# Splitting 544 token columns as 294 and 250, with one 500-column matmul per weight tile

## The chip, the cores and the metric

The kernel runs on one core of one Trainium2 chip. The metric is the device time of one execution in microseconds (us), median over runs. The engines are TensorE (PE for its matmuls, PEld for its weight loads), VectorE (DVE), ScalarE (ACT), GpSimd (POOL) and SyncE (SP), which issues the DMAs.

## The reference

One decoder layer is computed for 512 prompt tokens and 32 sampled tokens (8 sequences of 4), 544 columns in all. What matters here is that almost all of the work is products of the activations with large float32 weights, to float32 accuracy:

```
proj = rmsnorm(x) @ w_in                    # 2048 -> 4096: pooling inputs, q, k, v
pooled = pool_mix(u, ...)                   # windows 2/4/8/16, then @ w_pool
attn = moba(q, k, v, cache_k, cache_v)      # block-sparse attention, paged cache
x = x + rmsnorm(concat(pooled, attn) @ w_out)          # 2048 -> 2048
gt, up = h @ w_gate, h @ w_up               # h = rmsnorm(x), 2048 -> 5632 each
f = gelu(causal_conv3(gt)) * up
y = x + rmsnorm(f @ w_down)                 # 5632 -> 2048
```

## The kernel before, in words

Activations lie transposed: features on the 128 partitions, the 544 tokens along the free dimension. `act_hi[:, kt]` and `act_lo[:, kt]` hold, for each of 16 slabs of 128 features, the fp32r rounding of the activation and the fp32r rest. `f_hi` and `f_lo` do the same for four slabs of the FFN's inner activation.

Weights come in 724 *units* of 256 KB: two slabs (i = 0, 1) of 128 input features by 256 output features. SP loads a unit into a ring of four slots (`w_raw`). ACT rounds it to fp32r (`split_hi`, L255, into `w_hi`), and DVE subtracts to get the rest (`split_lo`, L261, into `w_lo`). Both run three units ahead of PE (`LEAD = 3`).

A *weight tile* is 128 by 128: a unit has four (i = 0, 1 and output halves mt = 0, 1). For each tile PE forms hi*hi + hi*lo + lo*hi. Each of the three products takes two matmuls of 272 token columns, one into each of two PSUM banks, so six matmuls a tile, each with its own weight load. `group` (L682) does this for the projections before the FFN, with all of mt = 0 before mt = 1 inside a unit. `ff_unit` (L705) does it for the FFN and for the first pair of groups, with i outermost.

A *group* is eight units, which finish 256 output features (mt = 0 and 1) in PSUM. Groups use the banks `ps_acc`, or for `odd = 1` the banks `ps_a` and `ps_b`. When a tile of a group is complete (`acc_done` for mt = 0, `unit_used` for mt = 1), DVE *evicts* it from PSUM to SBUF, mostly multiplied by `rstd`, and increments `acc_free`. PE waits on `acc_free` before the first matmul that overwrites these banks: the previous group's eviction (`prev=1`) where successive groups share `ps_acc`, the one before that (`prev=2`) where they alternate.

The stages in order:

- Input projection, 16 groups. The first two are interleaved (`pair_groups`). Groups 4 to 11 carry the score products with the cached keys between their units (L747), groups 12 to 15 the products with the cached values (L859). Between them stands the prompt attention.
- Four small pooling products, then the output projection: eight groups, evicted by `mix_tiles` (L1223). All but the first use `ps_acc` one after the other.
- The FFN: 11 chunks. A chunk has four gate/up groups (mt = 0 is the gate, mt = 1 the up projection), whose evictions are `gate_tail` (L1278 to L1301), and then 16 units of the down projection in four steps `down(d)`, whose results are added into `acc` (L1335, L1337). The chain of `gate_tail` goes from DVE to ACT and back three times (L599, L602, L606) and ends with `f_lo` (L1301), for which the down projection waits (`f_split`). Only then does DVE go on to the `split_lo` of the next group's fourth unit.
- Root mean square, residual, store.

The order on each engine is the program's order. The mean square of a normalisation (`sum_squares`, L716) is put into columns 272 to 407 of the `ps_acc` banks, beside group results that take columns 0 to 271.

## Time and profile before

| | |
|---|---|
| median of 3 runs | 2845.67 us (2845.61 to 2847.35) |
| span of the profiled execution, first to last instruction | 2843.8 us |
| left of the median around the span | 1.9 us |
| PE busy | 2740.9 us (96%), 19408 matmuls |
| DVE busy | 1172.0 us (41%) |
| ACT busy | 710.6 us (25%) |
| DMA | 122 GB/s over the span |

The profiled execution's own time is not given apart from its span; the runs shown are other executions, and their median is 1.9 us above the span. Busy shares of PE count overlapping matmuls once, and the end of a matmul is modelled, so the pace of matmuls is read from their starts.

### The profile page before, as it was taken

Reading aid. Unit: us, or ns where it says so; the run is one execution under the profiler, and the core shown is the slowest. Engines: PE = TensorE matmul, PEld = TensorE weight load, DVE = VectorE, ACT = ScalarE, POOL = GpSimd, SP = SyncE. Lnnn points to the kernel's source line nnn. Section 1 sums busy time; section 2 is a strip of 40 time slices with the busy share of each in tenths; the row PEclk is TensorE's granted clock in tenths of the full one; section 3 lists DMA queues with packets and bytes.
Section 4 is the critical chain, followed back from the end, with each engine's and each line's share of the span. In section 5 each row is a group of like instructions: output and inputs, shape, how many; then the busy total and the mean of one; then the engine's idle time right before and its main releaser. Section 6 shows DMA issues by size and latency. Waiting matters only on the chain.

```text
span 2843.8 us, 51136 instructions
## 1 busy us (share of the span) xinstructions
PE 2740.9 (96%) x19408; PEld 2416.9 (85%) x19408; DVE 1172.0 (41%) x1852; ACT 710.6 (25%) x1226; POOL 120.9 (4%) x265
## 2 busy tenths in 40 slices
PE   8999999979999999789999999999999999999994
PEld 8876767654444699789999999999999999999994
DVE  7433222340111433584343434444444343434357
ACT  5211111250111222342222222222222222222231
POOL 3000000000000000130000000000000000000002
PEclk9999999999999999899999999999999999999997
DMA  4455556407777442222222222222322223232321
GB/s 162 138 200 211 207 197 219 152 8 234 242 239 245 147 156 88 59 71 89 86 89 87 86 89 86 87 89 78 96 81 92 85 89 88 87 86 89 87 91 74
DMA packets 146616, 347.23 MB, mean 122 GB/s; under 512 B 16608, under 2 KB 16608, under 8 KB 146048
## 3 DMA queue, kind: packets, MB, share of 16 engines
q1 hardware_dynamic: 144480, 338.35, 37.2%
q0 software_dynamic: 2080, 8.14, 0.8%
q8 instruction: 35, 0.57, 0.1%
q14 instruction: 21, 0.17, 0.0%
HBM read 334.32 MB, written 12.10 MB: 122 GB/s over the span
## 4 chain that ended last, share of the span: by engine, by line
PE 93%; DVE 4%; DVEq 1%; ACT 1%; issue 0%; DMA 0%; POOL 0%; SPq 0%; ACTq 0%; POOLq 0%
PE ps_acc L705 28%; PE ps_acc L682 18%; PE ps_a L705 14%; PE ps_b L705 14%; PE ps_a L747 8%; PE ps_a L859 4%; PE ps_b L859 4%; PE ps_a L682 1%; PE ps_b L682 1%; PE ps_acc L801 1%; DVE act_lo L957 1%; DVE region L1362 0%; DVE w_lo L261 0%; DVE region L1247 0%; DVE region L1366 0%
## 5 line engine op out<-in xcount | busy, mean ns | idle before, releaser
L261 DVE TENSOR_TENSOR w_lo<-w_raw,w_hi 128x512 fp32r<-128x512 f32 x724 | 502.1, 705 | 1217.2 <-ACT w_hi L255 1214.2
L255 ACT ACTIVATE w_hi<-w_raw 128x512 fp32r<-128x512 f32 x724 | 445.5, 628 | 1397.7 <-PE ps_acc L682 475.9
L705 PE MATMUL ps_acc<-act_hi,w_hi 128*128 128x272 f32 x1472 | 308.4, 291 | 33.8 <-DVE act_lo L957 18.9
L705 PE MATMUL ps_acc<-act_lo,w_hi 128*128 128x272 f32 x1472 | 306.9, 290 | 0.0
L705 PE MATMUL ps_acc<-act_hi,w_lo 128*128 128x272 f32 x1472 | 304.8, 288 | 0.0
L682 PE MATMUL ps_acc<-act_hi,w_hi 128*128 128x272 f32 x1280 | 273.6, 295 | 2.0 <-DVE scratch L968 1.1
L682 PE MATMUL ps_acc<-act_hi,w_lo 128*128 128x272 f32 x1280 | 264.6, 288 | 0.0
L682 PE MATMUL ps_acc<-act_lo,w_hi 128*128 128x272 f32 x1280 | 263.9, 288 | 0.0
L705 PEld LDWEIGHTS ps_acc<-act_hi,w_hi 128*128 128x128 f32 x1472 | 232.5, 190 | 36.5 <-issue 22.1
L682 PEld LDWEIGHTS ps_acc<-act_hi,w_hi 128*128 128x128 f32 x1280 | 199.8, 188 | 49.7 <-issue 48.3
L747 PE MATMUL ps_a<-region,q_blk 128*32 128x256 f32 x1024 | 233.2, 382 | 2.3 <-ACT q_blk L423 2.3
L705 PEld LDWEIGHTS ps_acc<-act_hi,w_lo 128*128 128x128 f32 x1472 | 233.4, 190 | 0.0
L705 PEld LDWEIGHTS ps_acc<-act_lo,w_hi 128*128 128x128 f32 x1472 | 233.2, 190 | 0.0
L682 PEld LDWEIGHTS ps_acc<-act_lo,w_hi 128*128 128x128 f32 x1280 | 201.1, 189 | 0.0
L747 PEld LDWEIGHTS ps_a<-region,q_blk 128*32 128x32 f32 x1024 | 108.5, 110 | 108.2 <-ACT q_blk L423 2.5
L682 PEld LDWEIGHTS ps_acc<-act_hi,w_lo 128*128 128x128 f32 x1280 | 199.8, 189 | 0.0
L705 PE MATMUL ps_a<-act_hi,w_hi 128*128 128x272 f32 x736 | 153.4, 290 | 0.0
L705 PE MATMUL ps_b<-act_lo,w_hi 128*128 128x272 f32 x736 | 152.7, 288 | 0.0
L705 PE MATMUL ps_a<-act_lo,w_hi 128*128 128x272 f32 x736 | 152.3, 288 | 0.0
L705 PE MATMUL ps_b<-act_hi,w_lo 128*128 128x272 f32 x736 | 152.0, 288 | 0.0
L705 PE MATMUL ps_b<-act_hi,w_hi 128*128 128x272 f32 x736 | 151.7, 288 | 0.0
L705 PE MATMUL ps_a<-act_hi,w_lo 128*128 128x272 f32 x736 | 151.3, 286 | 0.0
(210 smaller groups left out, 3981.1 us busy)
## 6 DMA issues: line engine op xcount, KB each, us to landing
w_raw<-units SPq DMA_DIRECT2D x724, 256.0 KB, 2.6
region<-kcache SPq DMA_DIRECT2D x128, 512.0 KB, 4.2
region<-vcache SPq DMA_DIRECT2D x128, 512.0 KB, 4.5
region<-xT SPq DMA_DIRECT2D x8, 544.0 KB, 6.7
region<-xT SPq DMA_DIRECT2D x4, 1088.0 KB, 8.4
yT<-region SPq DMA_DIRECT2D x8, 544.0 KB, 2.7
ext_out<-region POOLq DMA_DIRECT2D x8, 339.5 KB, 4.5
kT_out<-scratch POOLq DMA_DIRECT2D x8, 272.0 KB, 5.8
```

What stands on the lines that cost most here:

```text
L255: act.activation(w_hi[:, s], w_raw[:, s], ACT.Copy).then_inc(hi_ready, 1)
L261: dve.tensor_tensor(w_lo[:, s], w_raw[:, s], w_hi[:, s].bitcast(F32), ALU.subtract).then_inc(lo_ready, 1)
L682: mm = pe.matmul(banks(mt, odd)[:, n, 0:HN], w[:, s, i, cols], half(a[:, kt], n), start=kt == 0 and w is w_hi and a is hi, stop=kt == 2 * ...
L705: mm = pe.matmul(banks(mt, odd)[:, n, 0:HN], w[:, s, i, cols], half(a[:, kt], n), start=kt == 0 and w is w_hi and a is hi, stop=kt == 2 * ...
L747: mm = pe.matmul(ps_a[0:HC, quad % 2, s * P:(s + 2) * P], q_blk[:, h * HC:(h + 1) * HC], pages[:, s:s + 2, h * P:(h + 1) * P], start=h == ...
L801: mm = pe.matmul(ps[:, 0, h % 2, kj * P:SEQ], v_tok[:, h, kj], probT[:, kj, kj * P:SEQ], start=kj == 0, stop=kj == 3)
L859: mm = pe.matmul(o[0:HC, n, :], p_seq[:, s % 2, c:c + HC], pages[:, slot, n * 512:(n + 1) * 512], start=pg == 0, stop=pg == PAGES - 1)
L957: dve.scalar_tensor_tensor(act_lo[:, kt], src[:, kt], g[:, kt:kt + 1], act_hi[:, kt].bitcast(F32), ALU.mult, ALU.subtract).then_inc(act_re ...
```

## The change

The columns are split as HA = 294 and HB = 250. `act_hi` and `act_lo` become the two halves of one tensor `act[:, kt, 0 or 1, :]`, so that columns 294 to 543 of the high and of the low part can be streamed by one matmul with 2 x 250 columns against `w_hi`. Its 500 results go side by side into the second bank. The first bank takes the 294 other columns in three matmuls as before. A fifth matmul adds `w_lo` times the high part of the 250 columns into the first 250 of the 500 sums. The second 250 (`b_rest`) are added when the tile is evicted. The interleaved first pairs of groups (32 units, where `sum_squares` needs its columns) and the four pooling products keep the six matmuls (`even=True`). That leaves 688 units with five.

```diff
+HA, HB = 294, 250
-        act_hi = sb("act_hi", [P, KT, NT], F32R)
-        act_lo = sb("act_lo", [P, KT, NT], F32R)
+        act = sb("act", [P, KT, 2, NT], F32R)
+        act_hi, act_lo = act[:, :, 0], act[:, :, 1]
+        rests = scratch[:, 3, 0:2 * HB].rearrange("p (m n) -> p m n", m=2)
+        def sums(mt, odd=0):
+            b = banks(mt, odd)
+            return b[:, 0, 0:HA], b[:, 1, 0:HB], b[:, 1, HB:2 * HB]
+        def products(pe, mt, odd, s, i, a, kt, first, last, even):
+            cols = slice(mt * P, (mt + 1) * P)
+            hi, lo = w_hi[:, s, i, cols], w_lo[:, s, i, cols]
...
+            bank_a, bank_b = banks(mt, odd)[:, 0, 0:HA], banks(mt, odd)[:, 1]
+            pe.matmul(bank_b[:, 0:2 * HB].rearrange("p (x n) -> p x n", x=2), hi, a[:, kt, :, HA:NT],
+                      start=first, stop=False)
+            pe.matmul(bank_a, hi, a[:, kt, 0, 0:HA], start=first, stop=False)
+            pe.matmul(bank_a, hi, a[:, kt, 1, 0:HA], start=False, stop=False)
+            pe.matmul(bank_a, lo, a[:, kt, 0, 0:HA], start=False, stop=last)
+            return pe.matmul(bank_b[:, 0:HB], lo, a[:, kt, 0, HA:NT], start=False, stop=last)
-                            for w, a in ((w_hi, hi), (w_hi, lo), (w_lo, hi)):
-                                for n in range(2):
-                                    mm = pe.matmul(banks(mt, odd)[:, n, 0:HN], w[:, s, i, cols], half(a[:, kt], n),
-                                                   start=kt == 0 and w is w_hi and a is hi,
-                                                   stop=kt == 2 * nu - 1 and w is w_lo)
+                            mm = products(pe, mt, odd, s, i, a, kt, kt == 0, kt == 2 * nu - 1, even)
+            def times_rstd(out, mt, odd=0):
+                (a, b, b_rest), rest = sums(mt, odd), rests[:, mt]
+                dve.tensor_tensor(rest, b_rest, rstd[:, HA:NT], ALU.mult)
+                dve.tensor_tensor(out[:, HA:NT], b, rstd[:, HA:NT], ALU.mult)
+                dve.tensor_tensor(out[:, 0:HA], a, rstd[:, 0:HA], ALU.mult).then_inc(acc_free, 1)
+                dve.drain()
+                dve.tensor_tensor(out[:, HA:NT], out[:, HA:NT], rest, ALU.add)
+            def times_rstd_spread(prompt, sample, mt, odd=0):
+                (a, b, b_rest), rest = sums(mt, odd), rests[:, mt]
+                dve.tensor_tensor(rest, b_rest, rstd[:, HA:NT], ALU.mult)
+                dve.tensor_tensor(prompt[:, HA:SEQ], b[:, 0:SEQ - HA], rstd[:, HA:SEQ], ALU.mult)
+                dve.tensor_tensor(sample, b[:, SEQ - HA:HB].rearrange("p (b l) -> p b l", b=DB), samples(rstd), ALU.mult)
+                dve.tensor_tensor(prompt[:, 0:HA], a, rstd[:, 0:HA], ALU.mult).then_inc(acc_free, 1)
+                dve.drain()
+                dve.tensor_tensor(prompt[:, HA:SEQ], prompt[:, HA:SEQ], rest[:, 0:SEQ - HA], ALU.add)
+                dve.tensor_tensor(sample, sample, rest[:, SEQ - HA:HB].rearrange("p (b l) -> p b l", b=DB), ALU.add)
...
-                    dve.tensor_copy(two(tile_of(acc, 2 * g + mt)), bank(mt, odd)).then_inc(acc_free, 1)
+                    t, (a, b, b_rest) = tile_of(acc, 2 * g + mt), sums(mt, odd)
+                    dve.tensor_copy(t[:, HA:NT], b)
+                    dve.tensor_copy(t[:, 0:HA], a)
+                    dve.drain()
+                    dve.tensor_tensor(t[:, HA:NT], t[:, HA:NT], b_rest, ALU.add).then_inc(acc_free, 1)
...
-                                    o = dve.tensor_tensor(two(t), two(t), bank(mt, i), ALU.add)
-                                o.then_inc(acc_free, 1)
+                                    dve.tensor_tensor(t[:, HA:NT], t[:, HA:NT], b, ALU.add)
+                                    dve.tensor_tensor(t[:, 0:HA], t[:, 0:HA], a, ALU.add)
+                                dve.drain()
+                                dve.tensor_tensor(t[:, HA:NT], t[:, HA:NT], b_rest, ALU.add).then_inc(acc_free, 1)
```

On PE, two weight tiles of the down projection (mt = 0 in `ps_a`, mt = 1 in `ps_b`; `f_hi`, `f_lo` and after the change `f_act` are the FFN's inner activation) stood like this before:

```order
L705 MATMUL ps_a<-f_hi,w_hi 128x272 x2
L705 MATMUL ps_a<-f_lo,w_hi 128x272 x2
L705 MATMUL ps_a<-f_hi,w_lo 128x272 x2
L705 MATMUL ps_b<-f_hi,w_hi 128x272 x2
L705 MATMUL ps_b<-f_lo,w_hi 128x272 x2
L705 MATMUL ps_b<-f_hi,w_lo 128x272 x2
```

and the same two tiles after it:

```order
L298 MATMUL ps_a<-f_act,w_hi 128x500
L300 MATMUL ps_a<-f_act,w_hi 128x294
L301 MATMUL ps_a<-f_act,w_hi 128x294
L302 MATMUL ps_a<-f_act,w_lo 128x294
L303 MATMUL ps_a<-f_act,w_lo 128x250
L298 MATMUL ps_b<-f_act,w_hi 128x500
L300 MATMUL ps_b<-f_act,w_hi 128x294
L301 MATMUL ps_b<-f_act,w_hi 128x294
L302 MATMUL ps_b<-f_act,w_lo 128x294
L303 MATMUL ps_b<-f_act,w_lo 128x250
```

Six matmuls of 272 columns became five with 500, 294, 294, 294 and 250: 1632 columns both times.

On DVE, the tail of a gate/up group (`scratch` holds the conv input, the conv result and the FFN buffer) stood like this before:

```order
L1278 TENSOR_TENSOR scratch<-ps_acc,rstd 128x272
L1279 TENSOR_TENSOR scratch<-ps_acc,rstd 128x240
L1280 TENSOR_TENSOR scratch<-ps_acc,rstd 128x8x4
L1286 TENSOR_TENSOR scratch<-ps_acc,rstd 128x544
L1289 SCALAR_TENSOR_TENSOR scratch<-scratch,region 128x560
```

and after the change:

```order
L998 TENSOR_TENSOR scratch<-ps_acc,rstd 128x250
L999 TENSOR_TENSOR scratch<-ps_acc,rstd 128x218
L1000 TENSOR_TENSOR scratch<-ps_acc,rstd 128x8x4
L1001 TENSOR_TENSOR scratch<-ps_acc,rstd 128x294
L1003 TENSOR_TENSOR scratch<-scratch 128x218
L1004 TENSOR_TENSOR scratch<-scratch 128x8x4
L989 TENSOR_TENSOR scratch<-ps_acc,rstd 128x250
L990 TENSOR_TENSOR scratch<-ps_acc,rstd 128x250
L991 TENSOR_TENSOR scratch<-ps_acc,rstd 128x294
L993 TENSOR_TENSOR scratch<-scratch 128x250
L1332 ISA
L1332 SCALAR_TENSOR_TENSOR scratch<-scratch,region 128x560
```

Four instructions ahead of the first step of the convolution became ten, with a drain inside each of the two parts.

## Rows read from the trace of the kernel before

**Rows 1.** Windows: busy us (count) of PE, PEld, DVE, ACT, POOL; granted clock; DMA.

```profile
122.00:445.00 323.00, 323.00 (x1930) 228.03 (x1928) 94.96 (x148) 52.48 (x94) 6.62 (x12) 1.00 0.59 205
640.00:1000.00 360.00, 359.54 (x1538) 186.26 (x1537) 76.19 (x119) 47.94 (x76) 4.31 (x8) 0.99 0.67 220
1000.00:1180.00 180.00, 176.06 (x1404) 175.64 (x1402) 63.81 (x92) 48.03 (x76) 0.00 (x0) 1.00 0.36 111
1312.00:2800.00 1488.00, 1488.00 (x11871) 1488.00 (x11870) 647.59 (x1044) 394.55 (x628) 24.93 (x159) 1.00 0.29 87
```

**Rows 2.** Chain that ended last: start us, length us, engine, tile, line, count.

```profile
1006.49 168.38 PE ps_acc L682 x1344
...
1645.08 24.12 PE ps_acc L705 x192
```

**Rows 3.** Window in the slow-clock start of the FFN: columns as in Rows 1.

```profile
1237.50:1240.30 2.80, 2.50 (x11) 2.53 (x12) 2.80 (x4) 0.21 (x1) 1.91 (x1) 0.50 0.24 83
```

**Rows 4.** Timeline of PE in that stretch.

```profile
1238.39 0.66 PE L705 MATMUL ps_acc<-act_lo,w_hi 128*128 128x272 f32 x2
1238.85 0.65 PE L705 MATMUL ps_acc<-act_hi,w_lo 128*128 128x272 f32 x2
1239.30 0.66 PE L705 MATMUL ps_acc<-act_hi,w_hi 128*128 128x272 f32 x2
```

**Rows 5.** Timeline of PE: the eight plain-float32 instructions of one sum of squares.

```profile
1248.01 1.09 PE L716 MATMUL ps_acc<-scratch,cst 128*128 128x136 f32 x8
```

**Rows 6.** Timeline of PE: value products of 512 columns, and the unit after them.

```profile
637.86 7.05 PE L859 MATMUL ps_a<-region,shared 128*32 128x512 f32 x16
...
645.20 0.41 PE L682 MATMUL ps_acc<-act_lo,w_hi 128*128 128x272 f32 x2
645.45 0.42 PE L682 MATMUL ps_acc<-act_hi,w_lo 128*128 128x272 f32 x2
645.70 0.41 PE L682 MATMUL ps_acc<-act_hi,w_hi 128*128 128x272 f32 x2
```

**Rows 7.** Groups by form: busy us, mean ns of one value product.

```profile
L859 PE MATMUL ps_a<-region,shared 128*32 128x512 f32 x256 | 112.9, 594 | 0.0
```

**Rows 8.** Timeline of PEld (weight loads), down projection.

```profile
1600.30 0.31 PEld L705 LDWEIGHTS ps_a<-f_hi,w_lo 128*128 128x128 f32 x2
```

**Rows 9.** Timeline of PE in that stretch: start us, length us, form, count.

```profile
1600.16 0.41 PE L705 MATMUL ps_a<-f_lo,w_hi 128*128 128x272 f32 x2
1600.41 0.41 PE L705 MATMUL ps_a<-f_hi,w_lo 128*128 128x272 f32 x2
```

**Rows 10.** Timeline of DVE: tail of one gate/up group, in brackets idle before it.

```profile
1668.48 0.44 DVE L1278 TENSOR_TENSOR scratch<-ps_acc,rstd 128x272 f32<-128x272 f32 x1 [0.91 <-PE ps_acc L705]
1668.84 0.40 DVE L1279 TENSOR_TENSOR scratch<-ps_acc,rstd 128x240 f32<-128x240 f32 x1
1669.15 0.18 DVE L1280 TENSOR_TENSOR scratch<-ps_acc,rstd 128x32 f32<-128x32 f32 x1
1669.47 0.72 DVE L1286 TENSOR_TENSOR scratch<-ps_acc,rstd 128x544 f32<-128x544 f32 x1
1670.65 0.80 DVE L1289 SCALAR_TENSOR_TENSOR scratch<-scratch,region 128x560 f32<-128x560 f32 x1 [0.46 <-ACT scratch L599]
...
1674.92 0.72 DVE L1301 TENSOR_TENSOR f_lo<-scratch,f_hi 128x544 f32 x1 [0.94 <-ACT f_hi L606]
1675.56 1.89 DVE L261 TENSOR_TENSOR w_lo<-w_raw,w_hi 128x512 fp32r<-128x512 f32 x3
```

**Rows 11.** Timeline of DVE: evictions of one output-projection group.

```profile
1053.25 0.72 DVE L1223 COPY region<-ps_acc 128x544 f32 x1 [0.27 <-PE ps_acc L682]
1054.76 0.72 DVE L1223 COPY region<-ps_acc 128x544 f32 x1 [0.78 <-PE ps_acc L682]
```

**Rows 12.** Timeline of DVE: the last evictions of the kernel.

```profile
2800.73 0.72 DVE L1337 TENSOR_TENSOR region<-region,ps_b 128x544 f32<-128x544 f32 x1
2801.64 3.19 DVE L1346 TENSOR_TENSOR scratch<-scratch 128x544 f32<-128x544 f32 x4 [0.19 <-issue]
```

More of the change, by code:

```diff
@@ L119, in build @@
         x2 = reg2[:, 0:KT * NT].rearrange("p (k n) -> p k n", k=KT)
-        f_hi = nc.alloc_sbuf_tensor_at("f_hi", [P, CH, NT], F32R, offset=base2 + 4 * KT * NT)
-        f_lo = nc.alloc_sbuf_tensor_at("f_lo", [P, CH, NT], F32R, offset=base2 + 4 * (KT + CH) * NT)
+        f_act = nc.alloc_sbuf_tensor_at("f_act", [P, CH, 2, NT], F32R, offset=base2 + 4 * KT * NT)
+        f_hi, f_lo = f_act[:, :, 0], f_act[:, :, 1]
         assert (KT + 2 * CH) * NT <= R2 and FT * NPAR <= R1 - KT * NT
@@ L281, in two @@
             return ap.rearrange("p (a n) -> p a n", a=2)
+        def sums(mt, odd=0):
[4 more added lines that the diff above has]
+            hi, lo = w_hi[:, s, i, cols], w_lo[:, s, i, cols]
+            if even:
+                for w, x in ((hi, 0), (hi, 1), (lo, 0)):
+                    for n in range(2):
+                        mm = pe.matmul(banks(mt, odd)[:, n, 0:HN], w, a[:, kt, x, n * HN:(n + 1) * HN],
+                                       start=first and w is hi and x == 0, stop=last and w is lo)
+                return mm
+            bank_a, bank_b = banks(mt, odd)[:, 0, 0:HA], banks(mt, odd)[:, 1]
[5 more added lines that the diff above has]
+            return pe.matmul(bank_b[:, 0:HB], lo, a[:, kt, 0, HA:NT], start=False, stop=last)
         @block.sync
@@ L664, in _, with group @@
         def _(pe):
-            def group(G, q, nu, hi, lo, ready=None, after=None, k0=0, first=False, odd=0, units=None, prev=1):
+            def group(G, q, nu, a, ready=None, after=None, k0=0, first=False, odd=0, units=None, prev=1, even=False):
                 for u in units or range(nu):
@@ L701, in ff_unit @@
                             pe.wait_ge(acc_free, 2 * G + mt + 1 - 2 * prev)
-                        cols = slice(mt * P, (mt + 1) * P)
-                        for w, a in ((w_hi, hi), (w_hi, lo), (w_lo, hi)):
-                            for n in range(2):
-                                mm = pe.matmul(banks(mt, odd)[:, n, 0:HN], w[:, s, i, cols], half(a[:, kt], n),
-                                               start=kt == 0 and w is w_hi and a is hi,
-                                               stop=kt == 2 * nu - 1 and w is w_lo)
+                        mm = products(pe, mt, odd, s, i, a, kt, kt == 0, kt == 2 * nu - 1, even)
                         if kt == 2 * nu - 1 and mt == 0:
@@ L759, in _ @@
             with pe.Fori(4, 8) as g:
-                group(g, 2 * g, 8, act_hi, act_lo, after=scores(g))
+                group(g, 2 * g, 8, act, after=scores(g))
             with pe.Fori(8, 12) as g:
-                group(g, 2 * g, 8, act_hi, act_lo, after=scores(g))
+                group(g, 2 * g, 8, act, after=scores(g))
                 pe.wait_ge(vt_out, 2 * g - 16 + 2)
@@ L886, in pool_product @@
                 f = 2 * (j % 2)
-                group(G_POOL + j, Q_POOL, 1, f_hi[:, f:f + 2], f_lo[:, f:f + 2], k0=K_POOL[j])
+                group(G_POOL + j, Q_POOL, 1, f_act[:, f:f + 2], k0=K_POOL[j], even=True)
             def ready2(u):
@@ L894, in _ @@
             pool_product(1)
-            group(G_OUT, Q_POOL, 8, act_hi, act_lo, ready2, first=True, odd=1, units=range(0, 4))
+            group(G_OUT, Q_POOL, 8, act, ready2, first=True, odd=1, units=range(0, 4))
             pool_product(2)
             pool_product(3)
-            group(G_OUT, Q_POOL, 8, act_hi, act_lo, ready2, first=True, odd=1, units=range(4, 8))
+            group(G_OUT, Q_POOL, 8, act, ready2, first=True, odd=1, units=range(4, 8))
             with pe.Fori(1, 8) as g:
-                group(g + G_OUT, 2 * g + Q_OUT, 8, act_hi, act_lo)
+                group(g + G_OUT, 2 * g + Q_OUT, 8, act)
             sum_squares(2 * KT)
@@ L921, in chunk @@
                     for k in range(4):
-                        ff_unit(2 * d + g0 + CH + k % 2, d + q0 + 2 * CH, k, k // 2, 2, f_hi, f_lo, k % 2,
+                        ff_unit(2 * d + g0 + CH + k % 2, d + q0 + 2 * CH, k, k // 2, 2, f_act, k % 2,
                                 f_ready if k % 2 == 0 else None)
@@ L1044, in _ @@
                     tile_done(dve, g, mt, 2 * g, 7)
-                    dve.tensor_tensor(two(stage[:, mt]), bank(mt), two(rstd[:, :]), ALU.mult).then_inc(acc_free, 1)
+                    times_rstd(stage[:, mt], mt)
                     dve.drain().then_inc(st_ready, 1)
```

60 lines of the change are left out of this document (33 added, 27 removed).

## The prediction

> **What bounds the kernel now.** I read the stages first [rows 1]: PE is busy for all of 122 to 445 us (input projection with keys), 640 to 1000 (with values) and 1312 to 2800 (FFN), and for 176 of 180 us in the output projection, while DVE and ACT are below half. The chain of waits agrees: whole groups of matmuls stand in it without a gap [rows 2]. So the pace of matmuls is the time, and the other engines matter only where PE comes to wait for them.
>
> That pace is the point. 1344 matmuls take 168.38 us [rows 2] and 11871 take 1488 us [rows 1]: 125.3 to 125.4 ns each. 272 columns at one a cycle of 2.4 GHz are 113.3 ns, so each loses 12 ns. What sort of loss? Three places bear on it.
>
> At a granted clock of 0.50 (the 1.2 GHz level) [rows 3] two matmuls take 0.453 us [rows 4], 226.7 ns each: exactly 272 columns at 1.2 GHz, no loss at all. A fixed cost put on every matmul would be there too; a floor that lies beside the streaming and is shorter than 227 ns would not. Eight plain-float32 instructions of 136 columns take 1.09 us [rows 5]; less the last one's own 0.28 (its neighbours' length) that is 7 gaps of 116 ns. Value products of 512 columns stand (7.05 - 0.594)/15 = 430 ns apart [rows 6, 7], 0.84 ns a column, so a plain instruction takes two cycles a column and 136 of them stream for the same 272 cycles. They go at 116, so neither the array nor a 128-column weight load by itself forces 125. And the load for a matmul starts when the matmul before it starts: the first of the w_lo pair is loaded from 1600.30 [rows 8], the matmul before it starts at 1600.16 + 0.125 = 1600.285, the matmul itself at 1600.41 [rows 9]. A load is never more than one matmul ahead.
>
> I read this as a floor: the fp32r chain of load and swap takes 125 ns, and a matmul takes the longer of that and its columns. It is an inference, and the rivals below are the other readings.
>
> **The change part by part.** *Matmuls.* Before, a tile takes 6 x 125.4 = 752.4 ns. After it the columns are the same 1632; there is one load less. No fp32r matmul of 500, 294 or 250 columns is in the trace. By the floor: 500 columns stream for 500 x 430/1024 = 210 ns, with the next load hidden; 294 stream for 123 and 250 for 105, so these four sit on the floor, 4 x 125.4 = 501.6. Sum 711.8, 40.6 less. From both sides: if columns alone count, 752.4 again and nothing saved; if the loss is 12.1 ns on each matmul, 740.3; if only streaming counts, 1632 x 0.42 = 685; and if the 250-column matmul, shorter than any of the fp32r ones shown, ran at the plain two cycles a column (210 ns), the floor's sum would be 85 higher, 796. I take 711.8, the reading that fits [rows 3 to 5] at once. 688 units of 4 tiles are 2752 tiles: -111.7 us. A unit goes from 3.01 us to 2.85.
>
> The Trainium skill ("TensorE: Matmul & The Clock Gate", section "Back-to-back issue gap") gives N/2.4 + 2.5 ns for an isolated warm matmul. By it six of 272 would be 695 ns and the five 692.5, so the change would be worth about 7 us. The trace has 125.4 where this gives 115.8, and the measurement decides.
>
> *Evictions.* DVE's length grows by (0.72 - 0.44)/272 = 1.03 ns a column [rows 10]: 250 columns 0.42 us, 294 0.46; back to back they start 0.34, 218 columns 0.31 and 32 0.11 apart. An inner drain I put at 0.1. Extra instructions on DVE cost nothing as long as it is done before PE needs it; there are three places to look at.
>
> The tail of a gate/up group. Before, the gate part takes from 1668.48 to 1669.33, ACT's step lets the convolution start 1.32 us later, at 1670.65, and the `split_lo` of the next group's fourth unit is done at 1675.56 + 0.7 = 1676.26 [rows 10]. After: 0.34 + 0.31 + 0.11 + 0.46 + 0.1 + 0.31 + 0.18 = 1.81 us for the gate part, against 0.85; then, beside ACT's 1.32, the up part with 0.1 + 0.34 + 0.34 + 0.46 + 0.1 + 0.34 = 1.68, so the convolution starts 3.49 us after the beginning, against 2.17. The whole tail behind it (two convolution steps, gelu, f_hi, f_lo, split) is 1.3 us later. PE starts the next group at 1645.08 + 24.12 - 0.16 (a last matmul's overhang) = 1669.04 [rows 2, 9] and its fourth unit 9.03 us later, at 1678.07. Slack 1.81 before; 1.32 with the shorter units; about nothing after the longer tail. I put 0.1 us on each of 31 such tails, 3 us.
>
> After the fourth group of a chunk the down projection needs the last `f_lo`. It is ready at 1674.92 + 0.72 = 1675.64, and PE is there two and a half units into the down part, at 1669.04 + 7.53 = 1676.57. Slack 0.93; 0.52 with shorter units; with the tail 1.3 later PE waits 0.8 us, 0.9 with the restart. 11 chunks: 10 us. Behind this waiting matmul stand all later matmuls of the chunk, so it counts in full.
>
> In the output projection successive groups share the banks. mt = 0 is evicted while PE does mt = 1, twelve matmuls or 1.5 us (the two copies are 1.51 apart [rows 11]), now ten or 1.42. The copy took 0.72; now two copies, a drain and an add from PSUM must be done: 0.34 + 0.46 + 0.1 + 0.42 = 1.32, plus 0.2 to 0.3 until DVE starts. PE waits about 0.4 us for 7 groups: 3 us. The groups with keys and values have their 7 us of score or value products [rows 6] between, the down steps alternate banks: nothing there. At the end the last two evictions are each 0.5 longer ahead of the sum of squares [rows 12]: 1 us.
>
> Sum: -111.7 + 3 + 10 + 3 + 1 = -95 us. The span of 2843.8 becomes 2749; the runs shown lie 1.9 us above it, so 2751.
>
> **The rivals.**
>
> *Slower: the fp32r rate limits, not the load.* If moving data come at 272/125.4 = 2.17 columns a ns at full clock, whatever the cuts, [rows 3] fits as well (1.2 is below 2.17), and plain matmuls move half the elements, so [rows 5] does too. Against it: there is no reason in the trace for such a rate. 1632 columns stay 752 ns, nothing is saved, and the waits remain: the last tails 1.3 - 0.93 + 0.1 = 0.5 x 11 = 5.5, the output projection 0.4 x 7 = 3, the end 1: 2855, slower. This mechanism decides as soon as a tile saves less than 9.5 us/2752 = 3.5 ns. In the same direction, and worse: with the 250-column matmul at two cycles a column a tile takes 796, 44 more than before, 44 x 2752 = 121 us, and with waits of some 10 us 2977.
>
> *A fixed loss per matmul.* 12.1 ns saved a tile, 33 us; waits of about 11 us (units 2.96): 2823. [Rows 4], with no loss at 1.2 GHz, speak against it unless the loss hides there.
>
> *Supply of instructions.* A matmul and its load are two instructions; if each takes 62.7 ns to hand over, five pairs take 627 and the tile streams for 685: 67 x 2752 = 185 us less. Units of 2.74 us turn the tails' slack to -0.3 and -1.1, and with the restarts waits come to 32 us: 2692. Against it: right after 16 value products of 430 ns each, through which the supply could run ahead, fp32r matmuls stand 0.25 a pair from the start [rows 6]. The Trainium skill (same page, section "Step-by-step: what each phase is for") puts the sequencer's work at about 62 ns per matmul in one mode, which is why this stays on the list; no run here shows the mode.
>
> **How the numbers follow.** Floor 0.52, supply 0.09, fixed loss 0.17, rate limit 0.13, slow 250-column matmul 0.06, 0.03 for none of these. Floor, fixed loss and supply are faster: 0.78 with a little taken off for waits that I sized too small. The rate limit gives slower, but within 0.2% (5.7 us) if its waits are half of mine: same 0.06, slower 0.16. About 0.2% is what a measurement of this kernel can tell from no change. The likeliest case by itself spans 2735 to 2775 (tile between 706 and 718 ns, waits 8 to 30 us). The range reaches from the supply's 2692 to just above the fixed loss at 2823: 2692 to 2830, which leaves out the rate limit and the slow matmul, 0.19, and the unknown.
>
> **What would show it.** In the changed profile, the starts behind a 500-column matmul should be 210 ns apart and the other four 125; 135 behind a 294 and 230 behind the 500 would be the rate limit, 12 more than the columns' time behind each the fixed loss, 123 and 105 behind the 294 and the 250 the supply. The chain of waits should show PE waiting for `f_act` from DVE once a chunk for about 0.8 us, and for `acc_free` 0.4 us in seven output groups. The forecast is wrong if a unit takes over 2.9 us, or if PE's waits in the FFN exceed 30 us.

## The result

The changed kernel takes 2853.53 us (median of 16 runs, 2850.94 to 2855.59); the kernel before, run beside it, 2847.36 (2845.53 to 2850.36). The ratio is 1.0021, interval 1.0013 to 1.0028: 6.2 us or 0.2% slower, where 2751 and a range of 2692 to 2830 were forecast. The profiled execution has a span of 2853.5 us at a mean granted clock of 0.984 of the full one, against 2843.8 at 0.986.

### The profile after

The windows of the FFN and of the output projection, columns as in [rows 1], which they answer to:

```profile
1000.00:1180.00 180.00, 179.75 (x1190) 169.50 (x1189) 69.12 (x118) 46.70 (x76) 0.00 (x0) 1.00 0.36 114
1312.00:2800.00 1488.00, 1484.37 (x9899) 1407.84 (x9898) 783.54 (x1633) 394.22 (x627) 25.53 (x163) 1.00 0.29 87
```

PE is as busy as before in the FFN: 1484 of 1488 us. It has 9899 matmuls in it instead of 11871, five sixths, and yet it does not get through sooner. So the five cost nearly what the six did. The timeline of PE in one tile of a gate/up group shows which (start us, length us, form, count; the matching rows of before are [rows 9]):

```profile
1699.95 0.39 PE L298 MATMUL ps_b<-act,w_hi 128*128 128x500 f32 x1
1700.18 0.29 PE L300 MATMUL ps_b<-act,w_hi 128*128 128x294 f32 x1
1700.31 0.30 PE L301 MATMUL ps_b<-act,w_hi 128*128 128x294 f32 x1
1700.45 0.30 PE L302 MATMUL ps_b<-act,w_lo 128*128 128x294 f32 x1
1700.58 0.28 PE L303 MATMUL ps_b<-act,w_lo 128*128 128x250 f32 x1
1700.70 0.39 PE L298 MATMUL ps_a<-act,w_hi 128*128 128x500 f32 x1
```

From start to start: 0.23 behind the 500, 0.13 to 0.14 behind each 294, 0.12 behind the 250. With waits left out, the means over all tiles of gate/up groups in the FFN are 224.3, 131.7, 140.0, 135.8 and 115.1 ns, together 746.9; in the down projection, which reads `f_act`, 227.9, 133.6, 135.3, 136.1 and 118.3, together 751.2. Before, six times 125.4 were 752.4 over the whole FFN.

Whole stretches of one chunk say the same. First the kernel before, then the changed one; in each a gate/up stretch of 128 tiles and the down projection of 64 behind it (the counts take in one to three matmuls that overhang an end):

```profile
1644.91:1741.35 96.44, 96.44 (x771) 96.44 (x769) 37.01 (x63) 25.78 (x41) 1.84 (x12) 1.00 0.29 87
1741.35:1789.35 48.00, 48.00 (x386) 48.00 (x385) 24.86 (x39) 11.97 (x19) 0.62 (x4) 1.00 0.28 88
```

```profile
1654.39:1749.98 95.59, 95.59 (x643) 90.97 (x641) 42.50 (x84) 25.79 (x41) 1.85 (x12) 1.00 0.29 88
1749.98:1798.66 48.68, 48.34 (x322) 45.58 (x321) 32.38 (x74) 11.98 (x19) 0.61 (x4) 1.00 0.29 85
```

Gate/up gains 0.85 us a chunk: 96.44/128 = 753.4 ns a tile became 746.8. The down projection loses 0.68. Its tiles were at 48.00/64 = 750.0 ns and are, without waits, at 751.2, so the pace gives it nothing. The rest of its loss is what the weight-load side of PE waits for in the FFN (total us, times, longest); before there was no such wait:

```profile
PEld ps_acc L298 <- DVE f_act L1344: 5.8, 11, 0.6
PEld ps_b L298 <- DVE region L1385: 0.5, 1, 0.5
```

Line 1344 is the subtraction that makes `f_lo`. The tail that leads to it, on DVE (start, length, form; idle before in brackets), answers to [rows 10]:

```profile
1677.75 0.42 DVE L998 TENSOR_TENSOR scratch<-ps_acc,rstd 128x250 f32<-128x250 f32 x1 [0.88 <-PE ps_acc L303]
...
1679.33 0.19 DVE L1004 TENSOR_TENSOR scratch<-scratch 128x32 f32<-128x32 f32 x1
1679.64 0.42 DVE L989 TENSOR_TENSOR scratch<-ps_acc,rstd 128x250 f32<-128x250 f32 x1
...
1681.18 0.80 DVE L1332 SCALAR_TENSOR_TENSOR scratch<-scratch,region 128x560 f32<-128x560 f32 x1
```

The convolution starts 1681.18 - 1677.75 = 3.43 us after the first eviction; before it was 2.17.

### The profile page after: what moved, and what is told of

Its sections match the earlier page's. It is cut to its first block, busy times and chain, and to the rows that moved or that the text cites. A ratio compares the mean times of both kernels' runs of the same rounds, so it can differ in the third digit from the quotient of the medians.

```text
span 2853.5 us, 46862 instructions
## 1 busy us (share of the span) xinstructions
PE 2743.4 (96%) x16656; PEld 2310.8 (81%) x16656; DVE 1340.9 (47%) x2572; ACT 711.2 (25%) x1226; POOL 122.0 (4%) x265
## 4 chain that ended last, share of the span: by engine, by line
PE 89%; DVE 6%; DVEq 2%; ACT 1%; issue 1%; DMA 0%; POOL 0%; SPq 0%; ACTq 0%; POOLq 0%
PE ps_acc L298 13%; PE ps_a L760 8%; PE ps_acc L301 8%; PE ps_acc L302 8%; PE ps_acc L300 7%; PE ps_acc L303 7%; PE ps_a L298 4%; PE ps_b L298 4%; PE ps_a L872 4%; PE ps_b L872 4%; PE ps_a L301 2%; PE ps_b L301 2%; PE ps_a L302 2%; PE ps_a L300 2%; PE ps_b L302 2%; PE ps_b L300 2%
## 5 line engine op out<-in xcount | busy, mean ns | idle before, releaser
L298 PE MATMUL ps_acc<-act,w_hi 128*128 128x500 f32 x1312 | 519.3, 396 | 4.1 <-DVE scratch L1319 1.8
L301 PE MATMUL ps_acc<-act,w_hi 128*128 128x294 f32 x1312 | 396.6, 302 | 0.0
L302 PE MATMUL ps_acc<-act,w_lo 128*128 128x294 f32 x1312 | 390.9, 298 | 0.0
L300 PE MATMUL ps_acc<-act,w_hi 128*128 128x294 f32 x1312 | 386.3, 294 | 0.0
L303 PE MATMUL ps_acc<-act,w_lo 128*128 128x250 f32 x1312 | 366.2, 279 | 0.0
L298 PEld LDWEIGHTS ps_acc<-act,w_hi 128*128 128x128 f32 x1312 | 249.1, 190 | 53.6 <-issue 50.4
L301 PEld LDWEIGHTS ps_acc<-act,w_hi 128*128 128x128 f32 x1312 | 246.2, 188 | 48.6
L303 PEld LDWEIGHTS ps_acc<-act,w_lo 128*128 128x128 f32 x1312 | 251.0, 191 | 0.0
L300 PEld LDWEIGHTS ps_acc<-act,w_hi 128*128 128x128 f32 x1312 | 248.0, 189 | 0.0
L302 PEld LDWEIGHTS ps_acc<-act,w_lo 128*128 128x128 f32 x1312 | 246.9, 188 | 0.0
L298 PE MATMUL ps_a<-act,w_hi 128*128 128x500 f32 x368 | 142.6, 387 | 1.0 <-DVE w_lo L263 1.0
L298 PE MATMUL ps_b<-act,w_hi 128*128 128x500 f32 x368 | 142.4, 387 | 0.0
L298 PE MATMUL ps_acc<-f_act,w_hi 128*128 128x500 f32 x352 | 138.4, 393 | 3.4 <-DVE f_act L1344 3.4
L872 PE MATMUL ps_a<-region,shared 128*32 128x512 f32 x256 | 112.9, 594 | 0.0
```

The source lines that it names most:

```text
L298: pe.matmul(bank_b[:, 0:2 * HB].rearrange("p (x n) -> p x n", x=2), hi, a[:, kt, :, HA:NT], start=first, stop=False)
L300: pe.matmul(bank_a, hi, a[:, kt, 0, 0:HA], start=first, stop=False)
L301: pe.matmul(bank_a, hi, a[:, kt, 1, 0:HA], start=False, stop=False)
L302: pe.matmul(bank_a, lo, a[:, kt, 0, 0:HA], start=False, stop=last)
L303: return pe.matmul(bank_b[:, 0:HB], lo, a[:, kt, 0, HA:NT], start=False, stop=last)
L872: mm = pe.matmul(o[0:HC, n, :], p_seq[:, s % 2, c:c + HC], pages[:, slot, n * 512:(n + 1) * 512], start=pg == 0, stop=pg == PAGES - 1)
```

## Experiments

The question was where the forecast's 112 us went: whether the five matmuls save little, and why, or save much and lose it to evictions. Times are medians; "before" is the kernel before, run on the same chip.

### p1: the pace by number of columns

The edit puts rows of matmuls behind the last sum of squares, for example

```diff
             sum_squares(4 * KT)
...
+            for t in range(32):
+                mm(A[:, 0:500], hs, x0[:, 0:500])
...
+            for t in range(32):
+                mm(A[0:32, 0:128], hs[:, 0:32], x0[:, 0:128])
```

> The six-matmul kernel, unchanged, with rows of fp32r matmuls behind its last sum of squares, 32 of a kind (512, 500, 500 in two pieces, 384, 294, 272, 256, 250, 224, 192, 128 columns, then 32-column weights, other banks, other weights), and 16 tiles each in the six-matmul order and in the five-matmul order; other engines are by then nearly idle. Its own length says nothing. Theory R (a rate with a small fixed part, the line 6.9 + 0.437 N ns through the four sizes of the changed kernel): 512 at 231, 500 at 225, 384 at 175, 272 at 126, 192 at 91, 128 at 63 to 65 ns, the same with 32-column weights; the tile 752 in six, 748 in five. Theory C (the 12 ns are contention of other engines and DMAs for on-chip memory): here 272 goes at 113 to 116 and 500 at 208 to 212. Theory W (the 128-column weight load takes cycles from the stream): with 32-column weights 272 goes at 113 to 116, with 128-column weights at 125. Theory F (my forecast's floor): nothing below 125. Theory S (the 500 pays for its two pieces, the 294 for three sums in a row in one bank): 500 in one piece at 212 to 216, in two at 225, and five matmuls with the bank changed each time some 25 ns a tile below the order of the changed kernel.

Start to start, ns: 512 columns 227, 500 in one piece 223, in two 229, 384 174, 294 133, 272 125.4, 256 119.5, 250 118, and 224, 192 and 128 all 111 (means of a row of 32). Windows over the 32 matmuls of 128 columns, then 272 and 128 columns with weights of 32 columns:

```profile
2899.35:2902.90 3.55, 3.55 (x35) 3.55 (x34) 0.00 (x0) 0.00 (x0) 0.00 (x0) 1.00 0.02 5
2902.90:2906.88 3.98, 3.98 (x34) 3.44 (x34) 0.00 (x0) 0.00 (x0) 0.00 (x0) 1.00 0.00 0
2906.88:2908.80 1.92, 1.92 (x35) 1.92 (x32) 0.00 (x0) 0.00 (x0) 0.00 (x0) 1.00 0.00 0
```

3.55/32 = 111 ns, 3.98/32 = 124.4, 1.92/32 = 60. So there is a floor, and it goes with the weights: with a quarter of their columns it falls from 111 to 60 or less. (Fewer weight columns are fewer output partitions too; that it is the load and not the output is argued, not shown.) But it lies at 111 ns, not at 125: 272 columns are above it, and stay at 124.4 with the short load. Contention with other engines (theory C) falls too: DVE, ACT, POOL and the DMAs stand at zero here and 272 columns still take 125. The tile took 751 in the order of six and 751 in that of five; changing the bank each time, with the long matmul in one piece, 750: theory S, which had some 25 less, falls. The Trainium skill ("TensorE: Matmul & The Clock Gate", section "LDWEIGHTS (loading the stationary operand)") gives a load as its columns divided by 1.2 in ns, whatever its rows, which makes an estimate of 106.7 for 128. The 111 and the 60 agree with that as a floor at the full clock; the 213.4 that p3 measures at the lower clock is twice the estimate.

### e1 and e2: the matmuls alone, the evictions alone

e1 keeps `products` as changed and puts back the evictions of before; e2 keeps the evictions as changed and puts back six matmuls:

```diff
 # e1, one of five places
-                    times_rstd(stage[:, mt], mt, odd)
+                dve.tensor_tensor(two(stage[:, mt]), bank(mt, odd), two(rstd[:, :]), ALU.mult).then_inc(acc_free, 1)
 # e2
-HA, HB = 294, 250
+HA, HB = 272, 272
-            return b[:, 0, 0:HA], b[:, 1, 0:HB], b[:, 1, HB:2 * HB]
+            return b[:, 0, 0:HA], b[:, 1, 0:HB], b[:, 0, 0:HB]
-            if even:
+            if True:
```

> Five matmuls per weight tile as changed, evictions as before the change (the 250 low-part columns are computed and not added, so that part of the result is left out). Theory R: 4.0 ns x 2752 tiles, -11 us against before (2836 where before is 2847), no waits for f_act beyond before's. Theory E (my forecast had the matmuls right in sign but evictions and waits ate a larger gain): -30 us or more. Theory N (five matmuls cost what six cost): 0, within 3 us.

> Six matmuls as before, with the changed kernel's evictions instruction for instruction (272, 272 and 272 columns in place of 294, 250 and 250; what is added is a sum that stands in another bank, so the result is not the reference's). Theory R: the evictions cost all of the difference and the matmuls' gain on top: about +17 us against before (2864). Theory N: +6 us (2853), the changed kernel's loss by itself. If the longer evictions were all hidden: 0.

e1: 2838.91 against 2847.4, ratio 0.9971 (0.9959 to 0.9982): -8.5 us. e2: 2862.16, 1.0053 (1.0039 to 1.0066): +14.8 us. Their sum, +6.3, is the changed kernel's +6.2. So the matmuls save 8.5 us, 3.1 ns a tile on the average, and the evictions cost 14.8. In e2's FFN the loads wait for the same line as in the changed kernel:

```profile
PEld ps_acc L294 <- DVE f_act L1344: 7.0, 11, 0.7
PEld ps_b L294 <- DVE region L1385: 0.6, 1, 0.6
```

### e3, e4, e5: the cut at 288 and 256

```diff
-HA, HB = 294, 250
+HA, HB = 288, 256
```

> The changed kernel cut as 288 and 256 instead of 294 and 250: the two-piece matmul is 512 columns, the total stays 1632. By the line 6.9 + 0.437 N the tile stays 748 ns and the time that of the changed kernel, 2853, within 3 us. If a matmul that fills its bank (512) or starts on a round column is cheaper, some 10 ns a tile: 2826. If the floor holds for anything: 250 to 256 changes nothing, 500 to 512 adds 5 ns a tile, 2867.

> The cut at 288 and 256 once more, for a profile at full clock. It took 2844.7 us where the cut at 294 takes 2853.5, 8.8 us or 3.2 ns a tile less. If the pace of the matmuls is the reason, the five starts in the FFN add up to 745 ns (748.3 at 294), and the waits for f_act stay at 0.5 us a chunk. If it is the evictions (lengths of 288 and 256 in place of 294 and 250, or other addresses), the five still add up to 748 and the waits are gone.

> Five matmuls cut at 288 and 256 with the evictions of before (256 columns of low parts are computed and not added, so that part of the result is left out): what the matmuls alone give at this cut. If the two effects add, the 2838.9 of the same at 294 less 8.8, 2830. If the cut at 288 gains by its evictions, 2839 again. If a fixed loss of 12 ns a matmul were all that counts, 2847 - 33 = 2814.

e3 took 2844.68, ratio 0.9989 (0.998 to 0.9998), and e5, with the old evictions, 2829.06, 0.993 (0.9916 to 0.9944). The columns are 1632 as ever, and the time is 9 to 10 us below that of the cut at 294 in both pairs, so it is the pace. In e4, one more execution of the same kernel for its profile (2843.92), a gate/up tile takes 740.0 ns, a down tile 753.4 without waits, and PE waits for `f_act` once a chunk as with the cut at 294. A fixed loss a matmul would have made every tile 740.3, so gate/up has now all that this rival promised, and the down projection nothing.

### p2, p4, p5: what sets the pace of a tile

p2 varies where the moving columns start, p4 their count in small steps, p5 the stretch that runs before; each has rows of tiles like

```diff
+            for t in range(32):
+                pe.matmul(B[:, 0:512].rearrange("p (x n) -> p x n", x=2), hs, act_hi[:, 0:2, 288:NT], start=True, stop=True)
+                pe.matmul(A[:, 0:288], hs, act_hi[:, 0, 0:288], start=True, stop=True)
+                pe.matmul(A[:, 0:288], hs, act_hi[:, 1, 0:288], start=True, stop=True)
+                pe.matmul(A[:, 0:288], ls, act_hi[:, 0, 0:288], start=True, stop=True)
+                pe.matmul(B[:, 0:256], ls, act_hi[:, 0, 288:NT], start=True, stop=True)
```

> As the first pace measurement (behind the six-matmul kernel, other engines idle), 48 of a kind, now with the start of the moving columns varied: 250 columns from column 0, 288, 294 and 2; 256 from 0 and 288; 272 from 0, 272 and 270; 288, 294, 304, 320 from 0; 500 and 512 in one piece and in two pieces; then 32 tiles each of the six, and of the five cut at 294, 288, 304 and 320, and at 294 and 288 with the long matmul in one piece. The loss is the pace less N/2.4 ns. Theory A (a piece that starts off a 32-byte or 64-byte boundary, as column 294 does at byte 1176 and column 288 at byte 1152 does not, costs 2 to 4 ns): 250 from 288 at 118 as from 0, from 294 and from 2 at 120 to 122; 500 in two pieces from 294 at 229, from 288 at 223; the five at 294 a tile of 750 to 753, at 288 of 742 to 746. Theory P (the second piece costs, wherever it starts): 500 and 512 in two pieces 6 ns over one piece at any start; the five 6 ns cheaper with the long matmul in one piece. Theory G (columns count in steps of 16 or 32): 294 costs what 304 or 320 costs, 250 what 256 costs, starts change nothing.

Timeline of PE in p2; a start less the start before it, divided by 48, is the pace. The rows are 272 columns from column 0 and from 272; 500 from 0 and from 294, 512 from 0 and from 288, all in one piece; 500 in two pieces from 294 and from 288:

```profile
2893.71 6.18 PE L949 MATMUL ps_a<-act_hi,w_hi 128*128 128x272 f32 x48
2899.72 6.24 PE L951 MATMUL ps_a<-act_hi,w_hi 128*128 128x272 f32 x48
...
2944.80 10.88 PE L965 MATMUL ps_a<-act_hi,w_hi 128*128 128x500 f32 x48
2955.53 11.05 PE L967 MATMUL ps_a<-act_hi,w_hi 128*128 128x500 f32 x48
2966.41 11.06 PE L969 MATMUL ps_a<-act_hi,w_hi 128*128 128x512 f32 x48
2977.31 11.35 PE L971 MATMUL ps_a<-act_hi,w_hi 128*128 128x512 f32 x48
2988.50 11.21 PE L973 MATMUL ps_a<-act_hi,w_hi 128*128 128x500 f32 x48
2999.54 11.24 PE L975 MATMUL ps_a<-act_hi,w_hi 128*128 128x500 f32 x48
```

125.2 for the 272; 223.5, 226.7, 227.1 and 233.1 for the next four; 230.0 for the 500 in two pieces. Less N/2.4 these lose 12, 15, 18, 14, 20 and 22 ns: the long matmul in two pieces loses 10 more than a 272, nearly the whole loss that one matmul less saves. But no theory holds through: 512 columns lose 20 from column 288 in two pieces and in one, and 250 or 272 columns from other starts lose only 1 more. The tiles took 753 (six), 747.2 (294), 740.8 (288), 741.5 (304), 743.9 (320). With the long matmul in one piece they took 747.0 (294) and 752.3 (288), so inside a tile the two pieces are not what costs.

> Behind the six-matmul kernel, other engines idle: 64 of each count from 264 to 352 columns from column 0, six counts from column 544, 288 columns from five other starts, and 32 tiles of five matmuls with the cut at 288, 290, 292, 294, 296, 298, 300, 304, 312 and 288 again. A tile cut at 294 took 747 ns and at 288 741 in the second pace measurement; this asks what sets the 6 ns. Theory A (starts off a 32- or 64-byte boundary cost): 288 from column 2, 4 or 8 at 134 to 136, from 0, 16 or 32 at 132; tiles 741 at cuts of 288, 296, 304, 312 and 746 to 748 at 290, 292, 294, 298, 300. Theory G (steps in the count of columns): the pace climbs in steps of 16 or 32 columns rather than 0.42 ns a column, the same from every start. Theory O (a loss of the order in the tile, of no regular cause that these rows show): tiles between 740 and 748 without a pattern in the cut.

The pace climbs by steps of a few ns (290, 292 and 294 columns all 133.4, 296 at 136.0), and 288 columns take 131.7 or 133.4 as the start is moved, without a rule by 32 or 64 bytes. The tiles: 753.2 at 288, 753.1, 748.5, 747.3 at 294, 740.5 at 296, 759.6 at 298, 750.1, 740.1 at 304, 751.0, and 753.4 at 288 again. The same tile of 288, with the same operands, had taken 740.8 in p2.

> Behind the six-matmul kernel, other engines idle: 32 tiles of five cut at 288, entered after 272-column matmuls, after 288-column ones from column 32, after 128-column ones, after tiles cut at 294, then the same with all moving operands 8, 4 and 16 columns (32, 16, 64 bytes) further on, and at last again from the first place before and after tiles of six. The same tile took 740.8 ns in one measurement and 753.2 in another. Theory O (the pace locks into one of two patterns by what came before): 741 or 753 by the entry, changing between the stretches with the same operands. Theory A (the address decides): all stretches with the same operands alike, and those shifted by 32 and 16 bytes the other one; then the difference between the two earlier measurements stays unexplained.

Windows over 32 tiles each, the rows shown all cut at 288 with the same operands: after 272-column matmuls, after 288-column ones, after 128-column ones, after tiles cut at 294, and the last after tiles moved by 64 bytes:

```profile
2859.03:2882.72 23.69, 23.69 (x163) 22.32 (x161) 0.00 (x0) 0.00 (x0) 0.00 (x0) 1.00 0.00 1
2891.25:2915.35 24.10, 24.10 (x162) 22.44 (x161) 0.00 (x0) 0.00 (x0) 0.00 (x0) 1.00 0.00 1
2922.45:2946.57 24.12, 24.12 (x162) 22.48 (x162) 0.00 (x0) 0.00 (x0) 0.00 (x0) 1.00 0.01 1
...
2970.49:2994.20 23.71, 23.71 (x163) 22.35 (x161) 0.00 (x0) 0.00 (x0) 0.00 (x0) 1.00 0.00 1
...
3065.94:3090.04 24.10, 24.10 (x163) 22.45 (x161) 0.00 (x0) 0.00 (x0) 0.00 (x0) 1.00 0.00 1
```

740, 753, 754, 741, 753 ns a tile, at full clock, with every other engine idle. Behind its first few tiles a stretch repeats itself, tile by tile or in a short cycle. The operands shifted by 32, 16 and 64 bytes took 748.1, 753.2 and 740.3. Two of the entries stand in an earlier run too and gave the same there: behind tiles cut at 294 740.8 (p2), behind 288-column matmuls from column 32 753.2 (p4). Theory O holds: a sequence of five falls into one of a few patterns, by how it is entered, and keeps it. These stretches also stand in different places of the program; e9 below rules that out as the whole cause. What inside PE or at its memory ports makes the pattern, no run here shows.

### p3: number of matmuls, and the lower clock

```diff
+            for t in range(64):
+                pe.matmul(A[:, 0:408], hs, x0[:, 0:408], start=True, stop=True)
...
+            pe.wait_ge(rested, 4)
+            for t in range(10):
+                pe.matmul(A[:, 0:272], hs, x0[:, 0:272], start=True, stop=True)
```

> Behind the six-matmul kernel, other engines idle: the same 1632 columns sixteen times as 4 matmuls of 408, 5 of 326 (1630), 6 of 272, 7 of 234 (1638), 8 of 204 and 12 of 136; then, each after some 20 us in which PE rests, ten matmuls of 128, 192, 250, 272, 294, 384, 500 and 512 columns. Theory L (a loss of about 12 ns on each matmul beside full-rate columns, and no matmul below 111 ns): a set takes 680 + 12 n, that is 728, 740, 752, 767 at full clock, then 888 (8 x 111) and 1332 (12 x 111). Theory R (a rate of 2.17 columns a ns): 752 for 4, 5, 6 and 7. At the 1.2 GHz level, where the first row of a burst should fall: if the loss is a fixed time, 272 columns at 239 ns and 128 at 119; if it is hidden there, as 226.7 ns in the rows of before say, 272 at 227, 250 at 208, 512 at 427 and 128 at 111 (the least time of a load) or 107.

Timeline of PE, sixteen sets of each:

```profile
2857.79 12.00 PE L939 MATMUL ps_a<-act_hi,w_hi 128*128 128x408 f32 x64
2869.62 12.22 PE L941 MATMUL ps_a<-act_hi,w_hi 128*128 128x326 f32 x80
2881.68 12.20 PE L943 MATMUL ps_a<-act_hi,w_hi 128*128 128x272 f32 x96
2893.72 12.70 PE L945 MATMUL ps_a<-act_hi,w_hi 128*128 128x234 f32 x112
2906.25 14.44 PE L947 MATMUL ps_a<-act_hi,w_hi 128*128 128x204 f32 x128
2920.53 21.57 PE L949 MATMUL ps_a<-act_hi,w_hi 128*128 128x136 f32 x192
```

A set takes 739 ns with four matmuls, 754 with five, 752 with six, 783 with seven, 893 with eight. Theory L had 728, 740 and 752 for the first three and theory R 752 for each: four lie between the two, five with R. From seven on the floor of 111 decides. Then the bursts after a rest; the granted clock of one is the number ahead of the last two in the windows row, 0.50, the 1.2 GHz level:

```profile
2967.60 2.40 PE L953 MATMUL ps_a<-act_hi,w_hi 128*128 128x128 f32 x10 [25.50 <-DVEq L1418]
...
3050.40 2.64 PE L962 MATMUL ps_a<-act_hi,w_hi 128*128 128x272 f32 x10 [25.10 <-DVEq L1418]
...
3161.18 4.41 PE L974 MATMUL ps_a<-act_hi,w_hi 128*128 128x512 f32 x10 [23.10 <-DVEq L1418]
```

```profile
3050.40:3053.00 2.60, 2.60 (x10) 2.32 (x10) 1.76 (x1) 0.00 (x0) 0.00 (x0) 0.50 0.00 0
```

After the first gap of a burst the single starts are 213.4 ns apart for 128, 192 and 250 columns, 226.7 for 272, 245 for 294, 320 for 384, 416.7 for 500, 426.7 for 512. That is N/1.2 from 272 up, without any loss, and below that a floor of 213.4: 256 cycles of that clock. At the full clock 256 cycles are 106.7, and the floor was 111. So the floor goes with the clock, and the loss of 10 to 22 ns was seen at the full clock alone.

### e6, e7, e8, e9: a version that beats both, and how firm its lead is

e8 is the cut at 288 with the addition for the up part put off behind the convolution; e6 has besides this the two pairs of banks in turn in the output projection; e7 is the kernel before with these banks alone; e9 is e6 with `f_act` moved.

```diff
 # e8 and e6
-                    times_rstd(f_buf, 1, odd)
+                    times_rstd(f_buf, 1, odd, add=False)
...
+                if not even:
+                    dve.tensor_tensor(f_buf[:, HA:NT], f_buf[:, HA:NT], rests[:, 1], ALU.add)
+                    dve.drain()
                 dve.wait_ge(gelu_done, F + 1)
 # e6, and so with its own evictions e7
-            with pe.Fori(1, 8) as g:
-                group(g + G_OUT, 2 * g + Q_OUT, 8, act)
+            group(1 + G_OUT, 2 + Q_OUT, 8, act, prev=2)
+            with pe.Fori(0, 3) as i:
+                for odd in (1, 0):
+                    group(2 * i + 3 - odd + G_OUT, 4 * i + 6 - 2 * odd + Q_OUT, 8, act, odd=odd, prev=2)
 # e9
-        f_act = nc.alloc_sbuf_tensor_at("f_act", [P, CH, 2, NT], F32R, offset=base2 + 4 * KT * NT)
+        f_act = nc.alloc_sbuf_tensor_at("f_act", [P, CH, 2, NT], F32R, offset=base2 + 4 * KT * NT + 32)
```

> The complete computation with the cut at 288 and 256, and two changes of order that shorten what PE waits for: in the tail of a gate/up group the 256 rest columns of the up part are added while ACT does the gelu, behind the convolution; and successive groups of the output projection use the two pairs of banks in turn, so that an eviction has a whole group's time. If waits cost what the traces show (5.6 us for f_act, 2.5 us in the output projection), 2844.7 - 4 - 2.5 = 2838, ahead of the kernel before at 2847.4. If DVE's extra 170 us cost elsewhere (splits late for PE), no better than 2844.

> The kernel before, with six matmuls and its own evictions, and only the banks of the output projection used in turn, as in the version with the late addition: does that version owe its lead to the order alone? Between the groups of the output projection the trace of before shows gaps of 0.1 us or less: 2847 less 1, the same as before. If the order alone were the reason, 2840 or less.

> The cut at 288 and 256 with the late addition in the tail of a gate/up group alone; the output projection keeps one pair of banks. The version with both took 2832.7, the cut alone 2844.7. By the waits seen in the traces the late addition should take 3.6 us off (f_act 5.1 to 1.4) and the banks the rest: 2841. If the late addition does more than the waits for f_act show, down to 2835.

> The version with the late addition and the banks in turn, with f_act 32 bytes further on, so that it starts on a 64-byte boundary as act does. In that version a tile of gate/up (from act) takes 740.0 ns and one of the down projection (from f_act) 753.4. Theory A (address): the 704 down tiles go to 740 too, 13.4 x 704 = 9.4 us less, 2823. Theory O (what comes before a stretch decides): the down tiles stay at 753, the time at 2832.7, or they change without a rule.

e6: 2832.67 us, ratio 0.9954 (0.994 to 0.9967), 14.7 below before. e7: 2847.36, 0.9999 (0.999 to 1.0008), so the banks alone give six matmuls nothing. e8: 2841.14, 0.9979 (0.997 to 0.9988): the late addition gave the 3.5 us that its waits had promised, the waits for `f_act` now being

```profile
PEld ps_acc L298 <- DVE f_act L1348: 1.9, 10, 0.2
```

The banks should have given 2 to 3 more and gave 8.5. The two profiles show where. First e8, then e6, from the last attention product of PE to the sum of squares behind the output projection:

```profile
971.60:1183.39 211.79, 207.63 (x1378) 193.77 (x1379) 91.41 (x154) 62.87 (x103) 0.00 (x0) 0.99 0.34 108
```

```profile
967.04:1174.76 207.72, 203.85 (x1379) 192.48 (x1379) 90.97 (x154) 62.84 (x103) 0.00 (x0) 0.99 0.35 110
```

4.1 us lie here: the waits at each change of group are gone, and the tiles between them, 746.2 ns in e8, take 740.0. Another 4.6 us lie ahead of this stretch, where both run the same instructions, and none behind it. Of these 4.6, 2.7 lie in the groups with keys, where the load side of PE has waits of 4.1 us in e8 and 1.0 in e6 for which the profile shows no cause; why they differ stays open. So about half of the lead over e8 can't be credited to the banks.

e9 shows how far the pace alone can move the time: 2845.97, 0.9994 (0.9985 to 1.0003), 13 us worse than e6 with 32 bytes moved. First e6, then e9, a gate/up stretch of 128 tiles and the down projection behind it:

```profile
1640.26:1734.98 94.72, 94.72 (x643) 89.29 (x641) 42.54 (x84) 25.77 (x41) 1.85 (x12) 1.00 0.32 89
1734.98:1783.43 48.45, 48.45 (x323) 45.23 (x321) 32.41 (x74) 11.96 (x19) 0.62 (x4) 1.00 0.29 86
```

```profile
1645.58:1741.44 95.86, 95.86 (x642) 89.86 (x641) 42.60 (x85) 25.80 (x41) 1.84 (x12) 1.00 0.30 88
1741.44:1789.65 48.21, 48.20 (x322) 44.97 (x321) 32.36 (x74) 11.97 (x19) 0.62 (x4) 1.00 0.30 86
```

The move did help the down projection, on average 749.0 in place of 753.5 a tile. But gate/up, whose operands were not moved, went from 740.0 to 748.9, and the output projection from 740.0 to 753.2, in both with the same instructions as in e6. That is the pattern of p5 in the kernel itself.

The ten such gate/up stretches of e9 are turns of one loop, the same instructions on the same addresses, and they do not agree: seven take 749 ns a tile, two 753 and one 740. One of the two, and the one:

```profile
1933.94:2030.37 96.43, 96.43 (x642) 89.78 (x641) 42.60 (x85) 25.79 (x41) 1.85 (x12) 1.00 0.30 87
2078.11:2172.83 94.72, 94.72 (x642) 89.34 (x641) 42.62 (x85) 25.77 (x41) 1.84 (x12) 1.00 0.30 89
```

So neither the place of the instructions nor the addresses can be the whole cause. What is left is the state in which a stretch is entered, and no run here shows what that state is. For the cut at 288 the best case is 740 for every tile and the worst 753: 13 x 2752 tiles is 36 us, more than twice what all the evictions cost.

## Why the prediction was wrong

*What bounds the kernel: right.* The pace of PE is the time; PE stayed full through the FFN.

*The floor: the step that failed.* The prediction read 125 ns as the least time of an fp32r load and swap, and had four of the five matmuls sit on it. A load and its matmul do have a least time, but it is 111 ns (p1), or 256 cycles (p3). The 272-column matmul lies above it, at 113 of streaming and 12 of loss. The 250-column matmul fell below the alleged floor at 115 to 118, and the 294 rose above it at 132 to 140. What misled was [rows 4]: no loss at the lower clock was taken to speak for a floor and against a loss on each matmul. p3 shows that the loss is absent at that clock for every size from 272 columns up, so those rows could not tell the two apart. [Rows 5], 116 ns for 136 plain columns, said that a load alone takes no more than 116; the 9 ns to 125 were put down to fp32r without a row. p1 also ends the rival of instruction supply: a load and its matmul stand 60 ns apart there, where it needed 62.7 for each of the two.

*The long matmul: 210 forecast, 224 to 228 measured.* It loses 16 to 20 ns, more than the 12 of a 272, and the 294 lose 9 to 18. That gives back half or more of the 12 ns which one matmul less can save. So the tile is 746.9 and 751.2 where the floor said 711.8, the rival of a fixed loss 740.3 and that of a rate 752.4. Neither rival is shown right: the rate fails on four matmuls of 408 (739), the fixed loss on five of 326 (754). The loss comes in patterns: at the cut of 288 a tile takes 740 to 753, at other cuts up to 759.6 (p4).

*The rate limit's 2855* is near the measured 2853.5, by offsets: it had no saving, where 8.5 us came, and waits of 9.5, where the evictions cost 14.8.

*The gate part and the tail: right.* 1.81 us forecast for the gate part, 1679.33 + 0.19 - 1677.75 = 1.77 measured; convolution start 3.49 forecast, 3.43 measured.

*Waits for f_act: right in place, too long.* 0.9 x 11 = 10 forecast, 5.8 measured, 0.5 each: the forecast counted on shorter units, and with a unit of 2.99 us the slack stayed. It is what the rate limit's sum had, 5.5.

*Tails of gate/up: 0.1 x 31 forecast, none seen.* No load in the FFN waits for `w_lo`.

*Output projection: 3 us forecast.* The waits of the load side for `acc_free` in it add up to 1.8 us:

```profile
PEld ps_acc L298 <- DVE region L1260: 1.8, 7, 0.4
```

Seven times and up to 0.4, as said, though most are shorter. From the last attention product to the sum of squares behind the projection PE takes 2.5 us longer than before, its tiles between the waits being no faster than 748.6.

*Missed:* a wait of 1.0 us for `w_lo` behind the third group of the input projection, where the split now stands behind longer evictions, 0.9 more for ACT's `q_blk` ahead of the first score product (3.2 in place of 2.3), and smaller delays. PE comes to the first score product 2.0 us later (119.1 in place of 117.1). The profiles, 9.7 us apart where the medians are 6.2 apart, have almost the whole loss ahead of the stretch between the FFN's two sums of squares: PE takes 2814.65 - 1257.47 = 1557.2 us for it, against 2804.89 - 1248.01 = 1556.9 before [rows 5]. There the saving and the waits cancel.

The sum of what the evictions cost, 17 forecast and 14.8 measured in e2, was the better half of the prediction, though its terms were off both ways: 10 for `f_act` were 7 in e2, 3 for the tails nothing, and the 2 of the input projection were not in it.

## What to carry to other kernels

When a matmul takes more than its columns, vary the column count by itself at the end of the kernel before building on a cause: one run gave the floor (111 ns with 128 weight columns) and the loss (10 to 22 ns) apart, where three readings of one size could not. Fewer and longer matmuls here saved about the loss of the one that went at best, and often less, since the others lost more; so what the evictions add must be priced against some 13 ns a tile at best and nothing at worst. And a difference of half a per cent between two such versions may be the pattern of the pace alone, or lie in stages that the edit does not touch: compare the start-to-start times of unchanged stages before an edit is given the credit.
